# Prompt attention: VectorE makes the low half of a turned chunk ahead of taking the next chunk of scores

## The reference

```python
s = jnp.einsum('bqhd,bkhd->bhqk', qblk, K, preferred_element_type=jnp.float32) * scale
s = s + fblk[..., None] - fkT                       # log forget gates, summed over time
mask = k_pos[None, :] <= pblk[:, None]
s = jnp.where(mask[None, None], s, -jnp.inf)
p = jax.nn.softmax(s, axis=-1)
return jnp.einsum('bhqk,bkhd->bqhd', p.astype(V.dtype), V)
```

## Time and profile before

| what | us |
|---|---|
| median of 3 runs (lowest, highest) | 1532.43 (1531.46, 2061.03) |
| profiled execution, its time | 1531.2 |
| its span | 1529.5 |
| TensorE busy, weight loads busy | 1479.1 (97%), 1310.3 (86%) |
| VectorE busy | 895.7 (59%) |
| ScalarE busy | 616.7 (40%) |
| GpSimd busy | 465.7 (30%) |

### The profile page before, as it was taken

The page is one execution under the profiler, slowest core; times in us unless marked ns, Lnnn a source line. Parts: engine busy times, 40 slices in busy tenths (PEclk is TensorE's granted clock), DMA queues, the critical chain, the costliest instruction groups (busy, mean ns, idle before and its releaser), DMA issues.

```text
span 1529.5 us, 23988 instructions
## 1 busy us (share of the span) xinstructions
PE 1479.1 (97%) x8828; PEld 1310.3 (86%) x8828; DVE 895.7 (59%) x2171; ACT 616.7 (40%) x1307; POOL 465.7 (30%) x675
## 2 busy tenths in 40 slices
PE   8999999999989999999999999999998999999999
PEld 8997888888869999999888889889887788777887
DVE  4333113343353352321789989988987788798663
ACT  5443021121121110100578778777876444433220
POOL 2110004555530020102344554454362455303221
PEclk9999999999999999999999999999999899999999
DMA  5533124434330020160645752663534566634442
GB/s 163 159 107 96 50 84 129 151 122 126 97 90 25 24 68 20 42 136 24 122 94 92 135 115 63 132 129 78 98 89 130 176 226 228 229 138 151 164 158 90
DMA packets 179462, 173.96 MB, mean 114 GB/s; under 512 B 72272, under 2 KB 137713, under 8 KB 176273
## 3 DMA queue, kind: packets, MB, share of 16 engines
q1 hardware_dynamic: 176832, 163.44, 38.7%
q10 hardware_dynamic: 2448, 8.91, 1.4%
q0 software_dynamic: 64, 0.07, 0.1%
HBM read 123.27 MB, written 49.12 MB: 113 GB/s over the span
## 4 chain that ended last, share of the span: by engine, by line
PE 54%; DVE 23%; issue 8%; POOL 7%; ACT 5%; DMA 2%; SPq 0%; DVEq 0%; ACTq 0%; POOLq 0%
PE banks L1071 18%; PE banks L1065 13%; PE banks L2678 7%; DVE pa_s_ring L1568 6%; DVE pa_pt_lo L1616 5%; POOL in_h_rstd L589 4%; POOL in_out L594 3%; PE banks L1657 3%; ACT pa_s_ring L1520 2%; PE banks L2127 2%; PE banks L2108 2%; PE banks L1673 2%; DVE sa_v_lo L2024 2%; PE banks L1674 2%; ACT pa_pt_hi L1543 2%
## 5 line engine op out<-in xcount | busy, mean ns | idle before, releaser
L1065 PE MATMUL banks<-in_w_hi,in_xt_hi 128*128 128x512 f32 (+1 forms) x680 | 243.0, 357 | 4.0 <-DVE in_w_lo L769 2.3
L1065 PE MATMUL banks<-in_w_hi,in_xt_lo 128*128 128x512 f32 (+1 forms) x680 | 237.8, 350 | 0.0
L1065 PE MATMUL banks<-in_w_lo,in_xt_hi 128*128 128x512 f32 (+1 forms) x680 | 237.2, 349 | 0.0
L1543 ACT ACTIVATE pa_pt_hi<-banks 128x512 fp32r<-128x512 f32 (+2 forms) x320 | 165.5, 536 | 91.6 <-PE banks L1657 91.2
L1616 DVE TENSOR_TENSOR pa_pt_lo<-banks,pa_pt_hi 128x512 fp32r<-128x512 f32 (+2 forms) x320 | 190.9, 605 | 12.2 <-ACT pa_pt_hi L1543 10.8
L1071 PE MATMUL banks<-in_xt_hi,in_w_hi 128*128 128x384 f32 (+1 forms) x576 | 193.7, 336 | 0.9 <-DVE in_w_lo L775 0.7
L1071 PE MATMUL banks<-in_xt_hi,in_w_lo 128*128 128x384 f32 (+1 forms) x576 | 189.8, 329 | 0.0
L1071 PE MATMUL banks<-in_xt_lo,in_w_hi 128*128 128x384 f32 (+1 forms) x576 | 189.5, 329 | 0.0
L1657 PE MATMUL banks<-ident,pa_s_ring 128*128 128x128 f32 x1088 | 173.3, 274 | 13.3 <-ACT pa_s_ring L1520 7.4
L1673 PE MATMUL banks<-pa_pt_hi,pa_vs 128*128 128x256 f32 x576 | 165.4, 303 | 4.3 <-DVE pa_parts L1596 3.7
L1520 ACT ACTIVATE pa_s_ring<-pa_s_ring,pa_least 128x1024 f32<-128x1024 f32 (+7 forms) x160 | 154.6, 966 | 0.0
(11 more groups left out here) (293 smaller groups left out, 2869.6 us busy)
## 6 DMA issues: line engine op xcount, KB each, us to landing
sa_k_c<-in_cache_k_dram SPq DMA_DIRECT2D x8, 2048.0 KB, 9.5
sa_v_c<-in_cache_v_dram SPq DMA_DIRECT2D x8, 2048.0 KB, 8.2
out_dram<-in_out SPq DMA_DIRECT2D x34, 256.0 KB, 2.1
out_dram<-op_x ACTq DMA_DIRECT2D x17, 512.0 KB, 3.4
scratch_qk_t<-in_t_hi SPq DMA_DIRECT2D x32, 256.0 KB, 2.6
scratch_qk_t<-in_t_lo SPq DMA_DIRECT2D x32, 256.0 KB, 3.0
pa_q_l<-scratch_qk_t SPq DMA_DIRECT2D x16, 512.0 KB, 13.3
pa_ks<-scratch_qk_t SPq DMA_DIRECT2D x16, 512.0 KB, 6.4
```

The source lines that it names most:

```text
L1065: mm = pe.matmul(ps[:, u % NBANK, 0:n], tile_of(xa, t)[:, k, :], wa[:, k, c0:c0 + n], start=(k == 0 and q == 0), stop=(k == KT - 1 and q = ...
L1543: act.activation(pt_hi[g % 2][:, b:b + nb, (j % 2) * P:(j % 2 + 1) * P], ps_t[:, turn_use(h, j, n) % 3, 0:nb * P].rearrange("p (b q) -> p ...
```

## The change

In each slot VectorE's two main pieces of work change places: it now makes the low half of chunk `(j, n)` first and then takes the scores of chunk `(j + 3, n)`. The inversion of row sums and the gating of an output keep their places behind both. No semaphore, count or buffer changes.

```diff
                 for n in range(slots):
-                    if n < n_take:
-                        take_chunk(*nxt, n)
                     if n < len(banks):
                         b, nb = banks[n]
                         dve.wait_ge(hi_done, h * NQD + q_before(j) + n + 1)
...
                                           ALU.subtract).then_inc(lo_done, 1)
+                    if n < n_take:
+                        take_chunk(*nxt, n)
                     if n == 0 and j % 2 == 0 and (j or h):
```

## The result

| kernel | median us | profiled execution's span |
|---|---|---|
| before | 1532.87 (1531.46 to 2061.03, 5 runs) | 1529.5 |
| changed | 1542.67 (1540.73 to 1545.60, 5 runs) | 1539.0 |

The ratio of the changed kernel to the one before is 1.0062, with a 95% interval from 1.0042 to 1.0082. One of the five executions before took 2061.03 us against 1534.54 or less for the others, and it is left out of the ratio.

The account below looks back on a forecast made before the run. TensorE and VectorE were taken to hold each other in turn. Per head 1.04 + 0.42 - 0.40 = 1.06 us, 8.5 for eight heads, gave a median of 1540.5 us, range 1529 to 1549.

Parts of the forecast that it names:

- VectorE's delay: Prompt attention: VectorE, waiting for ScalarE's high halves, late by 0.24, 0.57, 1.04, 1.34 us at steps 3, 5, 7, 9.
- The carrying through the gating: In steps 3 to 7, VectorE's late gating of outputs makes TensorE's value products equally late, 1.04 us a head.
- The wait for moved takes: Step 12: TensorE's score product waits 0.42 us for a take now second; part may fall on steps 10 and 11.
- The gain at step 13: Before step 13's first transpose, TensorE's 0.40 us wait for a low half of step 12 goes away.
- From step 13 to the head's end: ScalarE is the bound there, so what starts late ends late; with one take per step, order hardly matters.
- The sum: Per head 1.04 + 0.42 - 0.40 = 1.06 us slower; 8.5 us for eight heads of prompt attention.
- The signs named: Next profile: score waits below half of 17.4 us, high-half waits about 20, TensorE score-product waits about 0.4, heads 1.1 longer.
- Nothing happens: Rival: TensorE's gating waits are partly the profile's making and the lag is taken up; 0 to 3 us, chance 0.18.
- The ranking by occupancy: Skill's rule: VectorE, 49.4 of 54 us against 47.2, is the one to mend; work unchanged, time stays near 1532.
- Faster: Rival: delays at steps 3 to 7 don't arise, leaving only 0.40 us a head at step 13; 1529, chance 0.12.
- slower by more: Rival: the 0.42 us wait for a take recurs in each of steps 8 to 12; 13.4 us more, 1554, chance 0.10.
- The clock: Rival: TensorE's pauses drop its granted clock; one head at 1.2 GHz costs 52 us more, 1592, chance 0.02.

Follow-up runs that it names:

- The splits by slot and by step: Changed order kept only in part, against before: slot 0 1.0031, slots 1 and up 1.0055, steps 10 and up 0.9996, steps below 10 1.0069.
- the two fastest kernels: Kernel before with gating at start of slot 1 in odd steps below 12 (or 10), low half first from there: 53.76 us a head, 0.9987 (0.9986).
- The four steps alone: Kernel before with the low half first only in steps 3, 5, 7 and 9: 55.35 us a head, ratio 1.0071.
- the rest: Kernel before with the low half first in all steps but 3, 5, 7 and 9: 54.29 us a head, ratio 1.0009.

## Why the prediction was right

The direction, the size and the steps of the sum up to step 13 held; what was said of the stretch behind them did not. The forecast was 8.5 us. In prompt attention, from TensorE's first score (738.24 and 739.19) to the last copy of an output (1174.4 and 1184.0), the trace shows 8.65 us more. Another 0.95 us lies ahead of it, in the input part, which the change does not touch. A change of time outside prompt attention was named as a sign of being wrong. The first score starts anywhere from 737.82 to 740.39 in the thirteen kernels' profiles, whose input parts are the same, so 0.95 us are scatter and the sign was too strict.

- *VectorE's delay.* Steps 3, 5 and 7 were put at 0.24, 0.57 and 1.04 us and measured 0.25, 0.53 and 1.01. Step 9 was put at 1.34 and measured 1.29. The splits by slot and by step confirm that both sources are real.
- *The carrying through the gating*, the one cost that no row could price, was taken as whole. It is: TensorE's value product in step 8 is 1.01 us late, and the run with the gating moved up takes the whole cost back.
- *The wait for moved takes*, 0.42 us, was put on step 12. TensorE's delay grew from 1.01 to 1.44 us, 0.43, at that score, but nearly all of this came in steps 10 and 11, as the text had allowed.
- *The gain at step 13*, 0.40 us, measured 0.39 (from 1.50 us late to 1.11). The kernel with the change in steps below 10 alone, which keeps the wait, is only 0.13 us slower a head than the changed one, because it saves the waits for moved takes.
- *From step 13 to the head's end* the prediction had ScalarE as the bound: what starts late ends late, and the order hardly matters. This is the part that failed. TensorE's transposes are 1.11 us late at the start of step 13, 0.91 in its slot 3 and 1.24 at the start of step 14, where they wait for L(13,1) on VectorE. In the two fastest kernels, step 13 opens 0.71 and 0.42 us sooner than before and the heads end 0.34 sooner in both.
- *The sum*, 1.06 us a head, measured 1.10. That it fits this well is in part luck: it was closed with TensorE's delay at step 13 (1.11), while VectorE's lag, which sets the start of step 14, happened to be of nearly the same size (1.24 there).
- *The signs named.* The wait for scores was to fall below half and fell to 2.6 us. The wait for high halves was to rise to about 20 and rose to 32.8: I had counted only the waits that cost and not those of steps 1 and 2 (0.92 and 0.94 us a head), which took the place of waits for scores. Waits of 0.4 us on score products were foretold, and single ones are 0.2 at most.
- *The rivals.* "Nothing happens" fell: the waits marked at gatings were real and grew. The ranking by occupancy of the Trainium skill (Perfetto Trace Analysis, Identifying the Most-Contended Engine) names VectorE here. With VectorE's work unchanged the head took from 53.76 to 55.35 us by the order alone, so the time didn't stay where that rival had it. "Faster" fell: its 0.40 was real but smaller than the delay. In "slower by more" the wait for a take was to come back in five steps; it came in parts that sum to one. The clock stayed at 1.00, through more and longer waits of TensorE than before. The swings that the Trainium skill (TensorE: Matmul & The Clock Gate, A second HAM failure mode: psum-queue depth-cycling) tells of are not in this trace either.

## What to carry to other kernels

Where two engines hand work to each other through a few banks, the order on one of them is cover for the latency of a third: put the work whose input is ready first ahead, and the one that waits for a further hop behind it. Before moving a large instruction, look at the small ones behind it that release the other engine. Here a gating of 0.4 us, moved ahead of one take, took back the whole cost of the change.

A stretch has its own bound: the gating moved up won 0.22 us a head in steps 3 to 9 and put L(13,1) 0.40 us back in step 13, and only a split by steps showed it. Before counting a gain in the middle of a loop, ask what sets the loop's end: of 0.71 us won at step 13, 0.34 were left.

## What was not expected

Shares of steps do not add. The four steps alone cost 1.25 us a head, the rest 0.19, both together 1.10. A wait on one engine is lag that spares it the next, so leaving out the worst places moves the wait to the next one: in step 6, 0.23 us of waiting that the full change does not have.

Within one execution the lengths of heads 1 to 6 agree within 0.07 us, while whole executions of one kernel differ by 2 to 7 us, and those of the kernel before by up to 10 (1531.51 to 1541.29 beside one batch of experiments), and the parts outside prompt attention by up to 5 us between these kernels (from 354.9 to 359.8 us behind the last copy of an output). I did not look into why.
